# 64 bytes of unused space ahead of the weights' halves and 64 more ahead of the activations' operands, in a kernel of two transformer blocks

## What is computed

```python
# block 1
h = rms_norm(x, norm_mix);  u = h @ w_in            # 1024 -> 2560: lru_x, lru_g, q, k, v
y_lru = gelu(lru_g) * rg_lru(conv4(lru_x))          # gated linear recurrence
y_att = stick_breaking_attention(q, k, v)           # 8 heads of 64
x = x + concat(rms_norm(y_lru), rms_norm(y_att)) @ w_out
g, b = split(rms_norm(x) @ w_ffn_in)                # 1024 -> 2 * 2816
x = x + (silu(g) * b) @ w_ffn_out;  x = rms_norm(x)
# block 2
cb, cc, cin, q, k, v, f, gates = split(rms_norm(x) @ w_in_2)
y_conv = (cb * conv3(cc * cin)) @ w_out_conv_2
y_attn = forgetting_attention(q, k, v, cumsum(log_sigmoid(f))) @ w_out_attn_2
x = x + (sigmoid(gc) * y_conv + sigmoid(ga) * y_attn) @ w_o_2
a, b = split(conv3(rms_norm(x) @ w_up_2));  x = x + (silu(a) * b) @ w_down_2
out = rms_norm(x)
```

## Time and profile before

| | us |
|---|---|
| median of 2 runs (1365.08 to 1366.16) | 1365.62 |
| the profiled execution's own time | 1362.18 |
| its span | 1360.4 |
| TensorE matmul busy in the span | 1326.9 (98%) |
| VectorE busy | 777.6 (57%) |
| ScalarE busy | 510.3 (38%) |
| GpSimd busy | 108.3 (8%) |

### The profile page before, as it was taken

The page is one execution under the profiler, slowest core; times in us unless marked ns, Lnnn a source line. Parts: engine busy times, 40 slices in busy tenths (PEclk is TensorE's granted clock), DMA queues, the critical chain, the costliest instruction groups (busy, mean ns, idle before and its releaser), DMA issues.

```text
span 1360.4 us, 15770 instructions
## 1 busy us (share of the span) xinstructions
PE 1326.9 (98%) x6278; PEld 1074.5 (79%) x6278; DVE 777.6 (57%) x885; ACT 510.3 (38%) x575; POOL 108.3 (8%) x100
## 2 busy tenths in 40 slices
PE   7999999899999999997999999999999999999997
PEld 5777667688888889995888888767888888888886
DVE  7797654933333357876436433556676767664222
ACT  6463653412222235454212322464343334332122
POOL 4003010300000011224000001000310000000000
PEclk9999999999999999999999999999999999999999
DMA  5322001132222369541342222201322223232221
GB/s 167 123 93 93 32 1 62 62 123 93 92 92 92 123 150 270 105 101 49 125 155 93 93 93 93 93 1 43 112 93 92 93 92 112 73 123 93 75 96 62
DMA packets 103348, 130.35 MB, mean 96 GB/s; under 512 B 3338, under 2 KB 80378, under 8 KB 103170
## 3 DMA queue, kind: packets, MB, share of 16 engines
q1 hardware_dynamic: 97282, 115.99, 25.7%
q0 software_dynamic: 6000, 13.65, 5.1%
q10 hardware_dynamic: 16, 0.00, 0.0%
HBM read 127.52 MB, written 2.11 MB: 95 GB/s over the span
## 4 chain that ended last, share of the span: by engine, by line
PE 88%; DVE 5%; issue 3%; POOL 2%; ACT 2%; DMA 0%; ACTq 0%; SPq 0%; DVEq 0%; POOLq 0%
PE psum L1519 25%; PE psum L1521 25%; PE psum L1520 25%; PE psum L1637 3%; DVE w_lo L940 2%; PE psum L1664 2%; PE psum L1652 1%; POOL tmp L563 1%; PE psum L1789 1%; ACT w_hi L622 1%; PE psum L1790 1%; PE psum L1791 1%; PE psum L1847 1%; DVE act_lo L949 1%; DVE xT L1151 1%
## 5 line engine op out<-in xcount | busy, mean ns | idle before, releaser
L1519 PE MATMUL psum<-act_hi,w_hi 128*128 128x512 f32 x1224 | 485.7, 397 | 13.9 <-DVE act_lo L949 6.6
L1521 PE MATMUL psum<-act_hi,w_lo 128*128 128x512 f32 x1224 | 481.3, 393 | 0.0
L1520 PE MATMUL psum<-act_lo,w_hi 128*128 128x512 f32 x1224 | 477.6, 390 | 0.0
L622 ACT ACTIVATE w_hi<-raw 128x2048 fp32r<-128x2048 f32 (+1 forms) x102 | 192.4, 1887 | 590.6 <-PE psum L1521 579.6
L940 DVE TENSOR_TENSOR w_lo<-raw,w_hi 128x2048 fp32r<-128x2048 f32 (+1 forms) x102 | 233.7, 2291 | 126.8 <-ACT w_hi L622 126.8
L1519 PEld LDWEIGHTS psum<-act_hi,w_hi 128*128 128x128 f32 x1224 | 230.4, 188 | 70.3 <-issue 13.2
L1520 PEld LDWEIGHTS psum<-act_lo,w_hi 128*128 128x128 f32 x1224 | 230.3, 188 | 52.4 <-issue 1.4
L1521 PEld LDWEIGHTS psum<-act_hi,w_lo 128*128 128x128 f32 x1224 | 230.3, 188 | 51.3
L1789 PE MATMUL psum<-part_hi,w_hi 128*128 128x256 f32 x308 | 86.7, 282 | 1.3 <-DVE w_lo L940 1.3
L1790 PE MATMUL psum<-part_lo,w_hi 128*128 128x256 f32 x308 | 86.1, 279 | 0.0
L1791 PE MATMUL psum<-part_hi,w_lo 128*128 128x256 f32 x308 | 86.0, 279 | 0.0
(11 more groups left out here) (260 smaller groups left out, 1508.8 us busy)
## 6 DMA issues: line engine op xcount, KB each, us to landing
raw<-in_w_in SPq DMA_DIRECT2D x30, 1024.0 KB, 5.1
raw<-in_w_ffn_in SPq DMA_DIRECT2D x22, 1024.0 KB, 5.0
raw<-in_w_up SPq DMA_DIRECT2D x22, 1024.0 KB, 5.0
raw<-in_w_down SPq DMA_DIRECT2D x10, 1024.0 KB, 4.9
x_buf<-in_w_ffn_out POOLq DMA_DIRECT2D x6, 1024.0 KB, 10.1
raw<-in_w_out SPq DMA_DIRECT2D x4, 1024.0 KB, 4.9
raw<-in_w_o SPq DMA_DIRECT2D x4, 1024.0 KB, 5.1
x_buf<-in_w_ffn_out POOLq DMA_DIRECT2D x3, 768.0 KB, 10.6
```

What stands on the lines that cost most here:

```text
L622: A(w_hi[:, s % 2, 0:n], home(s, n), ACT.Copy).then_inc(w_hi_ready, 1)
L1519: mm(dst, stationary[0], moving[0], start=first, stop=False)
L1520: mm(dst, stationary[0], moving[1], start=False, stop=False)
L1521: return mm(dst, stationary[1], moving[0], start=False, stop=last)
```

## The change

Two tensors that nothing reads or writes are allocated, 16 fp32 elements (64 bytes) wide: one ahead of `w_hi`, one ahead of `act_hi`. No instruction is added, removed or put in another place. All that lies behind the first one starts 64 bytes later in its partition (`w_hi` at 49344, `w_lo`, `tmp`, `rstd`, `par`, the constants, `small`), and all that lies behind the second one 128 bytes later (`act_hi` at 104768, `hid_*` from 137536, `part_*`, `soft_*`, and every tensor that shares that space; `x_buf2` and the `y_buf`s follow through `act_base`). `xT` and `raw` stay where they were.

```diff
         xT = sb("xT", [P, DC, TOKENS])
         raw = sb("raw", [P, 2, SLAB])
+        sb("w_shift", [P, 16])
         w_hi = sb("w_hi", [P, 2, SLAB], F32R)
         w_lo = sb("w_lo", [P, 2, SLAB], F32R)
...
         eps = sb("eps", [P, 2])
         gain_both = sb("gain_both", [P, DC])
+        sb("act_shift", [P, 16])
         act_scope = ExitStack()
         act_base = nc.sbuf_base
         act_hi = sb("act_hi", [P, DC, TOKENS], F32R, act_scope)
```

## The result

The changed kernel takes 1376.95 us (2 runs, 1376.94 to 1376.96) against 1365.62: ratio 1.0083, 95% interval 1.0067 to 1.0100. So it is slower by 0.8%, where the forecast was no change (1365.1, range 1343 to 1388). The profiled execution took 1376.94 us with a span of 1375.2, 14.8 more than before. The kernel before scatters by some microseconds from run to run (1361.7 to 1366.9 in all its runs here), so the ratios carry 0.2% of uncertainty; the steps in the traces are far sharper than that. Its profiled execution was one of the short ones, 3.4 us under the median, and so the spans differ by 14.8 us where the medians differ by 11.3.

A forecast was written before the change was run, and what follows sets the result against it. TensorE's step between matmul starts was taken as the bound. Main form +2.0, seven products +0.3, last product and v -2.8, others nothing: -0.5 us on 1362.18, 1361.7; the median lying 3.4 higher, 1365.1, range 1343 to 1388.

The forecast's parts named there:

- That the address makes the two paces: Main form at 228.9 ns and last product at 233.3 were said to differ through their operands' start addresses.
- Parity as the coordinate: Starts sorted as even (multiple of 128 bytes) or odd (64 past); after the change all products become odd, odd.
- The probe: Suffix sums, already odd, odd, read as showing the products' later pace: about the main form's, +0.5 ns a matmul (-2 to +4).
- main form, +0.5 ns: Products of the main form, 3960 matmuls, each 0.5 ns slower: +2.0 us.
- Last product and v: Last product and slab of v, 720 matmuls, from 233.3 to 229.4 ns: -2.8 us.
- Seven products: 924 matmuls of 256 columns, same pair as the main form, +0.3 ns each: +0.3 us.
- Suffix sums: 96 matmuls, said to get the pair the main form had before the change: -0.05 us, nothing.
- rival 1: The stationary operand's parity decides: main form slows to 233.3 ns, last product unchanged; +19.4 us, 1385; chance 20%.
- Rival 2: The new spacing serves better: products' steps 2 to 3 ns under the main form's pace; -18.6 us, 1347; chance 17%.
- rival 3: The excess is a clash of the two reads and goes away: steps of 213.3 to 216 ns; -72 us, 1294; 6%.
- Rival 4: Operands at equal places in the 128 bytes collide more: products 7 ns a matmul slower; +33 us, 1398; 7%.
- Rival 5: Nothing happens: the operands' roles set the paces and each stage keeps its step; 1365.6; chance 12%.

The follow-up runs named there:

- w_only: 64 bytes of padding ahead of w_hi alone, against the kernel before; 1365.76 us, ratio 1.0014.
- act_only: 64 bytes of padding ahead of act_hi alone, against the kernel before; 1376.38 us, ratio 1.0091.
- act_128: 128 bytes of padding ahead of act_hi alone, against the kernel before; 1374.23 us, ratio 1.0076.
- act_192: 192 bytes of padding ahead of act_hi alone, against the kernel before; 1351.80 us, ratio 0.9898.
- both: 192 bytes of padding ahead of act_hi and 192 more ahead of part_hi, against the kernel before; 1348.82 us, ratio 0.9882.
- narrow: A kernel of its own: 512-column fp32r streams, stationary pieces cut to 128, 96, 64 and 32 columns; steps of 226.7 to 240.1 ns at 32.
- apart: A kernel of its own: starts of moving high, moving low and stationary low halves varied separately; 226.7 ns with all at 0, none of 64 triples better.
- stairs: A kernel of its own: moving operand cut to 452 to 512 columns; at distance 192, 220.0 ns with 500 columns and 228.8 with 504.

## Why the prediction was wrong

Held together, over all unbroken streams of each trace (distance in brackets, ns a step):

| kernel | main form | last product | seven products | us |
|---|---|---|---|---|
| before | 228.95 (64) | 233.35 (192) | 117.78 (64) | 1363 to 1366 |
| w_only | 228.90 (64) | 233.33 (192) | 117.78 (64) | 1365.76 |
| **the change** | 232.57 (128) | 232.72 (128) | 118.66 (128) | 1376.95 |
| act_only | 232.61 (128) | 232.35 (128) | 119.06 (128) | 1376.38 |
| act_128 | 233.33 (192) | 228.89 (64) | 113.97 (192) | 1374.23 |
| act_192 | 226.71 (0) | 226.67 (0) | 119.98 (0) | 1351.80 |
| both | 226.71 (0) | 226.67 (0) | 115.07 (192) | 1348.82 |

- **What bounds it**: right. The step is what moved, and by it 14.7 of the span's 14.8 us are accounted for.
- **That the address makes the two paces**: right; act_128 exchanges them between the stages.
- **Parity as the coordinate**: wrong. It described the two pairs there were, and a description by distance fitted as well. The text had the distance too (64 to become 128, which soft less neg_tri has already), so the choice of the probe did not hang on parity. Nor is the pace set by the addresses alone: the stream at 53.78 us of the kernel before had the main form's pair and 233.3 ns.
- **The probe**: this is the step that failed. The suffix sums do have distance 128. At the settled paces of this distance, 19.1 ns of excess with 512 columns (232.4), 12.0 with 256 (118.7) and 15.5 put between, their five steps would have 74 ns; the two low halves read 63 and 83, and the high half 50 where 67 would be due. So these steps scatter by more than the difference that they were asked about, and three readings of them were averaged into a pace. In fact they hardly read the distance at all: the same five steps take 0.81 to 0.83 us in the eight heads before, 0.81 to 0.82 after the change (distance 192), 0.82 in act_192 (64) and 0.81 to 0.84 in act_128 (0). Whether that is from the gap ahead of them or from their mixed lengths is not shown; no long stream of 384 columns was run. The term "main form, +0.5 ns" was +3.6: 14.3 us and not 2.0. The warning stood in the last lines and got no weight in the sum.
- **Last product and v**: forecast -2.8 us, measured -0.4. They went from one of the two slow distances (192) to the other (128), where they have both of its paces, 232.4 and 233.3. The same reading of the probe had put them at 229.4.
- **Seven products**: +0.3 forecast, +0.8 measured. Small, and in the right direction.
- **Suffix sums**: said to get the main form's pair. By distance they went to 192, not 64. The first and sixth start of the last head's low half went from 0.81 to 0.82 us apart, so it cost nothing.
- **VectorE, ScalarE, DMA**: nothing, as forecast.
- **Rivals**: rival 1 came nearest in size (+17.4 for the main form, +14.3 measured) and had the last product nearly right, for a wrong reason. Rival 2's step of some 226 ns exists, at distance 0, and rival 3's at no distance with fp32r. Rival 4, that equal places in the 128 bytes are the worst pair, is refuted by act_192, which has such a pair and the best paces with 512 columns. Rival 5, that the roles decide, is refuted by the change itself, which slowed the main form in the same role, and by act_128.

Open: why the distance counts. A clash that shrinks with the bytes of the load is excluded by narrow, one that depends only on each stream's start less that of the load beside it by apart, a plain rounding up to 16 columns by stairs. Other forms of a clash between the two reads are not excluded. What is seen is that many of the settled paces are whole or third multiples of 6.67 ns (226.7, 228.9, 233.3, 240.0), the time of 16 columns at the granted clock. The others are cycles: at 232.4 ns the single steps after the change run from 228 to 241 ns and repeat every seven, and seven take 1626.6 ns, 244 times 6.67; the 118.7 of the seven products repeats every five, 593.3 ns, 89 times 6.67. So these streams settle into cycles of a whole number of such times, and one distance can hold two of them. A mechanism for that was not found.

## What to carry to other kernels

In a kernel whose matmuls are fp32r, read the step between starts, per stage, and compare it with the columns' time; where it differs between stages of one shape, take moving start less stationary start modulo 256 bytes and try distance 0 for streams of 512 columns first. It cost one line and gave 1.0% between medians (0.75% between profiled spans), and with another distance for the 256-column streams 1.2% (1.0%). A few matmuls of mixed lengths behind a gap are no witness for the pace of a long stream, and bf16 and fp32 streams, at the 16 distances tried, need none of this.

## What the runs showed that was not expected

- The start addresses of the two operands set the pace of fp32r matmuls between 226.7 and 240.0 ns for 512 columns, with other engines at rest, and 4 bytes are enough (226.7 at distance 0, 238.0 at 4). It is not told in full by the distance: moving the low halves alone or narrowing the load changes it too.
- The same code at the same addresses has two paces, 113.3 or 117.8 ns with 256 columns at distance 192, 232.4 or 233.3 with 512 at distance 128, 228.9 or 233.3 at distance 64, and mostly keeps the one it fell into for a whole stretch (in both, one stretch changed behind a single step of 160 ns).
- Four columns more can cost 8.8 ns (500 to 504 at distance 192), and a narrower stationary piece can make the stream slower (231.1 with 32 columns, 228.9 with 128, at distance 64).
- With 512 columns bf16 pays 2.5 ns over its columns and fp32r 13.4 at the best.
